# Joined attention visits at equal distances in one decoder layer step

## What is computed

```python
def rms_norm(x, g):
    return x * lax.rsqrt(jnp.mean(x * x, axis=-1, keepdims=True) + 1e-6) * g

def prompt_layer(x, mem, ...):
    z = rms_norm(x, pre_g) @ w_in              # 1024 -> 3072, split in ten parts
    cb, cc, ch, cz, q, k, v, sz, mq, mz = jnp.split(z, points, axis=-1)
    y_conv = cb * short_conv(cc * ch, conv_w) * jax.nn.silu(cz)          # 384 channels
    # blocks of 128 queries on this and the previous 128 keys; 6 query heads, 2 kv heads
    y_swa = swa_attention(q, k_band, v_band, ..., sinks) * jax.nn.silu(sz)
    y_mem = mem_attention(mq, mk, mv) * jax.nn.silu(mz)                  # 4 heads, 256 memory tokens
    y = jnp.concatenate([y_conv, y_swa, y_mem], axis=-1) @ w_out
    return x + rms_norm(y, post_g), ...

def swa_attention(q, k, v, q_pos, k_pos, sinks):
    s = q k^T / 8 - slope * distance, masked to a window of 128
    p = softmax(concatenate([s, sink]))[..., :-1]
    return p v
```

## Time and profile before

| what | us |
|---|---|
| median of 3 runs | 873.94 (872.87 to 874.16) |
| profiled execution, its own time | 872.73 |
| its span, first to last instruction | 870.9 |
| PE busy | 861.3 |
| DVE busy | 470.8 |
| ACT busy | 243.9 |
| POOL busy | 601.1 |

### The profile page before, as it was taken

How to read it: one execution, slowest core, us unless ns; L and a number is a source line. 1 busy time by engine, 2 the same in 40 slices (tenths; PEclk the granted TensorE clock), 3 DMA queues, 4 the chain that set the end, 5 groups by cost and what they waited for, 6 DMA issues and landing times.

```text
span 870.9 us, 13723 instructions
## 1 busy us (share of the span) xinstructions
PE 861.3 (99%) x5228; PEld 709.9 (82%) x5228; DVE 470.8 (54%) x1007; ACT 243.9 (28%) x672; POOL 601.1 (69%) x809
## 2 busy tenths in 40 slices
PE   8999999999999999999999999999999999999997
PEld 8999999998887877777887778777777887787785
DVE  4346688867252527864624346775444053687514
ACT  5433223312121441331311323332121133133111
POOL 4699666439968757727979756653787985776771
PEclk9999999999999999999999999999999999999999
DMA  9457322208357222213646432220543632222242
GB/s 321 177 187 235 103 69 74 74 6 305 126 174 261 98 97 97 73 49 109 256 163 227 171 115 97 65 81 13 181 155 118 232 113 80 73 73 73 58 161 96
DMA packets 38641, 114.01 MB, mean 131 GB/s; under 512 B 6000, under 2 KB 12400, under 8 KB 38160
## 3 DMA queue, kind: packets, MB, share of 16 engines
q1 hardware_dynamic: 37856, 112.02, 37.2%
q10 hardware_dynamic: 720, 1.12, 0.4%
HBM read 103.89 MB, written 10.25 MB: 131 GB/s over the span
## 4 chain that ended last, share of the span: by engine, by line
PE 87%; issue 7%; POOL 4%; DMA 1%; DVE 0%; ACT 0%; SPq 0%; DVEq 0%; POOLq 0%; ACTq 0%
PE pj L646 62%; PE pa L646 22%; POOL w_lo L599 2%; PE pa L798 1%; POOL w_hi L596 1%; PE pa L761 1%; DMA w_raw<-in_weights 1%; POOL rstd L617 1%; PE pa L679 0%; ACT diag L1020 0%; SPq L451 0%; POOL w_lo L611 0%; DVE o_nat L1618 0%; DVEq L244 0%; PE pa L729 0%
## 5 line engine op out<-in xcount | busy, mean ns | idle before, releaser
L599 POOL TENSOR_TENSOR w_lo<-w_raw,w_hi 128x256 fp32r<-128x256 f32 x516 | 411.0, 827 | 10.8
L646 PE MATMUL pj<-h_hi,w_hi 128*128 128x512 f32 (+2 forms) x936 | 337.4, 361 | 2.7 <-POOL w_lo L611 1.7
L646 PE MATMUL pj<-h_hi,w_lo 128*128 128x512 f32 (+2 forms) x936 | 328.6, 351 | 0.0
L646 PE MATMUL pj<-h_lo,w_hi 128*128 128x512 f32 (+2 forms) x936 | 328.0, 350 | 0.0
L596 POOL TENSOR_SCALAR w_hi<-w_raw 128x512 fp32r<-128x512 f32 x258 | 170.1, 677 | 149.7 <-PE pj L646 130.4
L646 PEld LDWEIGHTS pj<-h_hi,w_hi 128*128 128x128 f32 x936 | 176.4, 188 | 39.5 <-issue 17.1
L646 PEld LDWEIGHTS pj<-h_hi,w_lo 128*128 128x128 f32 x936 | 176.4, 188 | 23.5
L646 PEld LDWEIGHTS pj<-h_lo,w_hi 128*128 128x128 f32 x936 | 176.7, 189 | 20.6
L646 PE MATMUL pa<-w_hi,y_hi 128*128 128x512 f32 x160 | 63.8, 398 | 0.0
L646 PE MATMUL pa<-w_lo,y_hi 128*128 128x512 f32 x160 | 62.4, 390 | 0.0
L646 PE MATMUL pa<-w_hi,y_lo 128*128 128x512 f32 x160 | 62.3, 389 | 0.0
(11 more groups left out here) (216 smaller groups left out, 1062.5 us busy)
## 6 DMA issues: line engine op xcount, KB each, us to landing
...
```

What stands on the lines that cost most here:

```text
L599: last = pool.tensor_tensor(w_lo[slot][:, part], raw[:, part], w_hi[slot][:, part].bitcast(F32), ALU.subtract)
L646: return pe.matmul(out, lhsT, rhs, start=start, stop=stop)
```

## The change

The tables of steps change: scores stand at 27, 43, 59, 75 (16 more in quarter 0), so 16 steps apart; both kinds of transposes stand in one visit 9 steps behind (`ATT_T`); the values stand 16 steps behind, which is the step of the next block's scores, and so values of block i and scores of block i+1 are one visit. `nat_turn` moves into the first visit of transposes and writes the right halves of `pa[0]` and `pa[1]` (its sample part `pa[2]`); ACT copies them out in two halves after the block's `mem_pt`. `mem_values` writes `pa[3]` in place of `pa[4]`. `spread_rstd` of the next quarter moves from behind the first output tile into the last visit of values; its means, `diag` and the waits for them move from the third to the second group of convolution tiles. `first_sums` shrinks from 16 matmuls to 2, since DVE adds the eight squares first with four instructions. The count of warm-up matmuls ahead of the first projection stays at 17, over three banks in place of two. `diag` gets memory of its own.

```diff
@@ -200,15 +200,14 @@
-ATT_S = {(q, i): (27, 45, 61, 77)[i] + (16 if q == 0 else 0) for q in range(NQ) for i in range(NBLK)}
-SW_T = {key: s + 8 for key, s in ATT_S.items()}
-MM_T = {key: s + 9 for key, s in ATT_S.items()}
-ATT_V = {key: s + 13 for key, s in ATT_S.items()}
+ATT_S = {(q, i): (27, 43, 59, 75)[i] + (16 if q == 0 else 0) for q in range(NQ) for i in range(NBLK)}
+ATT_T = {key: s + 9 for key, s in ATT_S.items()}
+ATT_V = {key: s + 16 for key, s in ATT_S.items()}
 SM_S, SM_T, SM_V, SM_O = 10, 16, 19, 22
...
-WARM = 9
+WARM = 5
 ROWS_AT = 5
@@ -326,9 +325,8 @@
         x_row = sb("x_row", [P, D])
-        tanh_at = nc.sbuf_base
         tanh_t = sb("tanh_t", [P, 2, TP])
-        diag = at_("diag", [P, TH], tanh_at)
+        diag = sb("diag", [P, TH])
@@ -365,7 +363,8 @@
         row_loaded, res_loaded, xs_loaded, mt_loaded = sems("row_loaded res_loaded xs_loaded mt_loaded")
-        ones_set, x_squares, x_sums, first_his, xts_loaded = sems("ones_set x_squares x_sums first_his xts_loaded")
+        ones_set, x_squares, x_added, x_sums, first_his, xts_loaded = sems(
+            "ones_set x_squares x_added x_sums first_his xts_loaded")
         w0_loaded, w_pieces, k_split, kept, gated = sems("w0_loaded w_pieces k_split kept gated")
@@ -665,23 +664,14 @@
             def nat_turn(q):
-                if q == SAMPLE_OUT + 1:
-                    pe.wait_ge(s_mean, 1)
                 wait_used(pe, (q, "V0", len(chunks(q)) - 1))
+                pe.wait_ge(sw_max, 3 * NBLK * q + 3)
+                for b in range(NBLK):
+                    last = pe.transpose(pa[b // 2][:, (2 + b % 2) * P:(3 + b % 2) * P], v_raw[:, b * P:(b + 1) * P], ident[:])
                 if q == 0:
-                    wait_used(pe, (0, "Q0", 1))
-                if q:
-                    pe.wait_ge(free_dve, FREE_DVE[q - 1, "O0", out_blocks(q - 1) - 1])
-                for b in range(NBLK):
-                    last = pe.transpose(pa[2][:, b * P:(b + 1) * P], v_raw[:, b * P:(b + 1) * P], ident[:])
-                if q == 0:
-                    pe.wait_ge(kept, 1)
                     for g in range(2):
-                        last = pe.transpose(pa[3][0:TG, g * P:(g + 1) * P], v_raw[:, TP + g * TG:TP + (g + 1) * TG],
+                        last = pe.transpose(pa[2][0:TG, (2 + g) * P:(3 + g) * P], v_raw[:, TP + g * TG:TP + (g + 1) * TG],
                                             ident[:])
@@ -732,7 +722,9 @@
                     wait_used(pe, (q, "Q2", len(chunks(q)) - 1))
-                    pe.wait_ge(nat_out, q + 1)
+                    if q == SAMPLE_OUT + 1:
+                        pe.wait_ge(s_mean, 1)
                     if q:
@@ -763,6 +755,8 @@
                 pe.wait_ge(sw_pt, 3 * (NBLK * q + i + 1))
+                if i == 0:
+                    pe.wait_ge(nat_out, q + 1)
                 for kt in range(2):
@@ -805,7 +799,7 @@
                         a = (2 * p + hh) * HD
-                        last = mm(pa[4][HALF_OF[hh], 0:2 * P], mv_sb[:, kt, a:a + HD],
+                        last = mm(pa[3][HALF_OF[hh], 0:2 * P], mv_sb[:, kt, a:a + HD],
                                   mpt[:, hh, kt, :, :].rearrange("p a b -> p (a b)"), kt == 0, kt == 1)
@@ -857,11 +851,9 @@
+                pe.wait_ge(x_added, 1)
                 for b in range(2):
-                    for k in range(KT):
-                        if b == 0 and k % 2 == 0:
-                            pe.wait_ge(x_squares, k // 2 + 1)
-                        last = mm(pa[4][:, b:b + 1], x_sq[:, k, b * P:(b + 1) * P], ones[:, 0:1], k == 0, k == KT - 1)
+                    last = mm(pa[4][:, b:b + 1], x_sq[:, 0, b * P:(b + 1) * P], ones[:, 0:1], True, True)
                 last.then_inc(x_sums, 1)
@@ -886,7 +878,6 @@
                         pe.wait_ge(kept, 2)
-                        pe.wait_ge(nat_out, 1)
                     rows = slice(b * P, (b + 1) * P)
@@ -923,7 +914,7 @@
                     elif b == 3:
-                        pe.wait_ge(mm_pt, 2 * NBLK * (q + 1))
+                        pe.wait_ge(mm_y32, NBLK * (q + 1))
                     else:
@@ -948,7 +939,7 @@
             pe.wait_ge(ones_set, 1)
-            for a in range(2):
+            for a in range(3):
                 for c in range(4):
@@ -974,8 +965,6 @@
                             sample_sums()
-                        if s == 9 and q or s == 21 and q == 0:
-                            nat_turn(q)
                         if q in (1, 2):
@@ -989,9 +978,13 @@
                                 mem_values(q, i)
-                            if s == SW_T[q, i]:
+                                if i == NBLK - 1 and q + 1 < NQ:
+                                    spread_rstd(4, 0, TP, 0, 3 + q + 1)
+                            if s == ATT_T[q, i]:
+                                if i == 0:
+                                    nat_turn(q)
                                 swa_turn(q, i)
-                            if s == MM_T[q, i]:
                                 mem_turn(q, i)
@@ -1009,10 +1002,6 @@
                             out_tile(q, half, kp, b)
-                        if half == 0 and o == 0 and q + 1 < NQ:
-                            pe.wait_ge(mm_y32, NBLK * (q + 1))
-                            spread_rstd(4, 0, TP, 0, 3 + q + 1)
@@ -1093,12 +1082,16 @@
+                act.wait_ge(sw_pt, 3 * NBLK * q + 3)
                 if q:
...
                     for g in range(2):
-                        copy(vn_t[g][:], pa[3][0:TG, g * P:(g + 1) * P])
-                copy(v_sb[:, 1:1 + NBLK, :, :].rearrange("p b v d -> p (b v d)"), pa[2][:]).then_inc(nat_out, 1)
+                        copy(vn_t[g][:], pa[2][0:TG, (2 + g) * P:(3 + g) * P])
+                for a in range(2):
+                    last = copy(v_sb[:, 1 + 2 * a:3 + 2 * a, :, :].rearrange("p b v d -> p (b v d)"), pa[a][:, 2 * P:4 * P])
+                last.then_inc(nat_out, 1)
@@ -1229,17 +1222,15 @@
                             diag_of("m", 0, 2)
-                        if q + 1 < NQ and name == "CB2" and part == 1:
-                            wait_gate(act, (q, "CZ2", len(chunks(q)) - 1))
+                        if q + 1 < NQ and name == "CB1" and part == 1:
+                            act.wait_ge(spread, 3 + q)
                             diag_of(q + 1, 0, NBLK)
...
                             memory_values()
-                        if s == 9 and q or s == 21 and q == 0:
-                            values(q)
                         if q in (1, 2) and s == SM_S:
@@ -1248,8 +1239,10 @@
                                 mem_y_hi(q, i)
-                            if s == MM_T[q, i]:
+                            if s == ATT_T[q, i]:
                                 mem_pt(q, i)
+                                if i == 0:
+                                    values(q)
                             if s == ATT_S[q, i]:
@@ -1572,7 +1565,7 @@
                 wait_gate(dve, (q, f"Z{3 + p}", len(chunks(q)) - 1))
-                dve.scalar_tensor_tensor(out=mo_sum[:], in0=pa[4][:, 0:2 * P], scalar=0.5,
+                dve.scalar_tensor_tensor(out=mo_sum[:], in0=pa[3][:, 0:2 * P], scalar=0.5,
                                          in1=gate[:, 3 + p, gr * 2 * P:(gr + 1) * 2 * P], op0=ALU.mult,
@@ -1654,6 +1647,11 @@
+            for i in range(1, 4):
+                dve.wait_ge(x_squares, i + 1)
+                need(step(dve.tensor_tensor(x_sq[:, 0:2, :], x_sq[:, 0:2, :], x_sq[:, 2 * i:2 * i + 2, :], ALU.add)))
+            dve.tensor_tensor(x_sq[:, 0, :], x_sq[:, 0, :], x_sq[:, 1, :], ALU.add).then_inc(x_added, 1)
             for k in range(KT):
@@ -1713,7 +1711,7 @@
                                 sample_y(q)
-                        if q + 1 < NQ and name == "CH2" and part == 3:
+                        if q + 1 < NQ and name == "CH1" and part == 3:
                             means_of(q + 1)
```

## The result

The changed kernel takes 865.3 us (median of 4 runs, 865.27 to 865.56), the kernel before 873.7 us (4 runs, 872.9 to 874.2): a ratio of 0.990, with a 95% interval of 0.989 to 0.991. The forecast was 863.3 us, range 861.0 to 869.0. The profiled execution of the changed kernel has the median's time, 865.29 us, and a span of 863.5 us, where the kernel before had 872.73 and 870.9: 7.4 us less in the traces, 8.4 in the medians, 10.6 forecast.

The account below looks back on a forecast made before the run. PE, busy 99% of the span, was taken to bound the kernel. Gains of 3.0 + 1.6 + 2.5 + 0.4 + 0.6 + 1.7 + 0.8 = 10.6 us gave 863.3 us as median, range 861.0 to 869.0.

Parts of the forecast that it names:

- sums on PE: Start phase: four one-column passes in place of 32, additions ready on DVE at 19.1 us; 3.0 us gained.
- clock behind the sums: Start phase: the stretch at half clock behind the one-column passes goes; 1.6 us gained, 0 if the clock still falls.
- values with scores: Twelve joined visits: each saves the exit of the values, 0.21 us; 2.5 us gained, bounds 0 and 3.6.
- transposes and V: Sixteen joined visits of transposes, V's in four of them; 0.4 us gained in all, bounds -1 and +1.
- spread in the values' visit: `spread_rstd` in the last visit of values saves one exit in three quarters; 0.6 us gained, bounds 0 and 1.
- POOL's wait at CB2: Means come 16 steps earlier, so PE no longer waits for POOL's late split at CB2; 1.7 us gained, bounds 1.0 and 1.8.
- late normalising: Memory transposes of block 2 no longer catch DVE's last product, in four visits of quarters 1 to 3; 0.8 us gained.
- sums that start by 19.6 us: Start phase, a sign the forecast holds: PE's one-column row with about 0.4 us, starting by 19.6 us.
- late scores behind `o_sum`: Joined visits, a sign of being wrong: first scores over 0.15 us behind `o_sum`'s end minus its cover by memory values.
- Rival 1: DVE's products, slowed by POOL's splits, come late for the transposes in blocks 2 and 3: 4.8 us, 868.1 us; chance 0.15.
- Rival 2: Start gives less: additions take the upper end, clock falls nevertheless; 866.1 us. Chance 0.10 including joints that cost their saving.
- Rival 3: Joined visits of values and scores count as idle and lower PE's clock: 19 us, 882.5 us; chance 0.06.

Follow-up runs that it names:

- experiment 2: The changed kernel with the old sums, 16 matmuls of one column on PE and no additions on DVE: 868.45 us, ratio 0.9935 to the kernel before.
- experiment 5: The changed kernel with the values 13 instead of 16 steps behind the scores, so two visits again: 867.09 us, ratio 0.992 to the kernel before.
- experiment 6: The changed kernel with the window's transposes (and V's) one step ahead of the memory's, splitting the joined visits: 865.56 us, ratio 0.9905 to the kernel before.
- experiment 10: The kernel before with one line changed, DVE making the next quarter's means at CH1, not CH2: 872.41 us against 873.71, ratio 0.998.
- experiment 11: The changed kernel with DVE's `o_sum` of quarter 0 ahead of the second chunk's evacuation: 865.16 us, ratio 0.990 to the kernel before.
- experiment 7: The changed kernel with 56 more wait instructions on PE ahead of the first projection, no more work: 865.57 us, ratio 0.990 to the kernel before.
- experiment 9: The changed kernel with DVE's final rows in quarter 3 held until PE is done with tile K0: 863.94 us, ratio 0.989 to the kernel before.
- experiment 1: The changed kernel run again with no edit: 865.07 us, ratio 0.990 to the kernel before.
- experiment 12: The changed kernel with `o_sum` of quarter 0 ahead of the second evacuation and quarter 3's final rows held until K0 is done: 863.43 us, ratio 0.9883.
- experiment 3: The changed kernel with one DVE addition of 1024 columns and 8 sums on PE: 865.31 us, ratio 0.990 to the kernel before.
- experiment 4: The changed kernel with DVE's four additions behind the first three `h_lo` of the second chunk: 865.48 us, ratio 0.991 to the kernel before.
- experiment 8: The changed kernel with DVE's final rows of the quarter before at step 9 instead of 5: 865.45 us, ratio 0.990 to the kernel before.

## Why the prediction was right, and where it was not

The direction, the order of the terms and most sizes held; the time came out 2.0 us above the forecast. By its terms, as forecast and as measured in the traces:

| term | forecast | measured | from |
|---|---|---|---|
| sums on PE | 3.0 | 3.1 | after, experiment 2 |
| clock behind the sums | 1.6 | 1.5 | experiment 2 |
| values with scores | 2.5 | 2.6 | rows of both traces (0.20 each); experiment 5 (0.23 each) |
| transposes and V | 0.4 | 0.3 | experiment 6, without V |
| spread in the values' visit | 0.6 | 0.0 | below |
| POOL's wait at CB2 | 1.7 | 1.7 | experiment 10 |
| late normalising | 0.8 | 0.8 | four visits 0.20 us shorter; experiment 6 |
| start later | 0 | -0.9 | after, below |
| `o_sum` late in quarter 0 | 0 | -0.8 | after, experiment 11 |
| Q0 of quarter 3 | not seen | -1.2 | experiments 7, 9 |

The measured terms make 7.1 us, the traces show 7.4; 0.3 us I can't place, and the joints alone are open by that much (0.20 or 0.23 us, twelve times).

**Sums.** The step that failed is not their size. The prediction worked out when the additions would be ready (19.1 us; it was 16.9, for they began 2 us earlier and took 3.7 against 4.0) and asked whether PE would wait for them. (Its 0.4 us for handshakes stands in no row; the four additions follow each other without a visible gap.) It said itself that POOL splits beside them, and took the slow price for DVE from that, but left out POOL's half of the same collision. PE waits for POOL there. Its own sign for this, sums that start by 19.6 us, failed: 20.43. The 0.9 us are a net figure. From the first projection to the sums PE took 1.4 us more than before, and began 0.5 us earlier. Of the 1.4, 0.8 are the additions' (the two distances of 0.42 and the 0.22 behind each); 0.5 stand ahead of them (0.32 us at 11.32 and 0.50 at 12.56), beside DVE's own `w_lo`, which began 1.7 us earlier than before; 0.1 is a longer wait for weights. Six traces with the additions and the clock at 1.00 in this phase (after, experiments 1, 5, 9, 11 and 12) take 9.7 to 10.3 us from the end of the wait for weights to the sums, the kernel before 9.0. There is only one such trace without the additions, and in the executions whose clock fell in this phase the stretch takes 10.2 to 10.3 us with them (experiments 3, 4, 6 and 8) and without (experiments 2 and 10). So the place is shown, and the size is good to some tenths.

**Values and scores.** The price of 0.21 us for each, from the exit alone, was right to 0.02. It was split otherwise than it came out: the distance from the memory part of the values to the next thing is 0.97 us in the joined visit and was 0.96 ahead of a projection, so what went is the 0.11 behind the values and the 0.09 in front of the scores. The cover of `o_sum` was worked out for one chunk of 512 columns and counted twelve times; in quarter 0 it is another sequence, with the second chunk's two products ahead. That is the mis-sized term: two places of the kind "each us of lateness costs one", 0.12 and 0.65 us. The prediction had named late scores behind `o_sum` as a sign of being wrong, and there it came.

**Spread.** Forecast: "saves one exit in three quarters, 0.2 x 3". The trace of after, last values of quarter 1, and of before, behind the first output matmul:

```profile
395.59 1.13 PE L645 MATMUL pa<-diag,ones 128*128 128x512 f32 x2
396.15 0.80 PE L645 MATMUL pj<-h_hi,w_hi 128*128 128x512 f32 x1
396.78 0.39 PE L645 MATMUL pj<-h_lo,w_hi 128*128 128x512 f32 x1
```

```profile
206.04 1.02 PE L646 MATMUL pa<-diag,ones 128*128 128x512 f32 x2
206.49 0.80 PE L646 MATMUL pa<-w_hi,y_hi 128*128 128x512 f32 x1
207.13 0.40 PE L646 MATMUL pa<-w_lo,y_hi 128*128 128x512 f32 x1
```

The dear part is the distance behind the spread, 0.63 us, and it moved with it; 0.56 inside the visit against 0.45 alone is the 0.11 behind the values that I had counted as saved, and the 0.10 at their end stayed here as well. Above what PE would need without the spread this is 0.56 + 0.63 - 0.34 = 0.85 us after and 0.45 + 0.64 - 0.23 = 0.86 us before.

**Rivals.** Rival 1 (DVE late for the transposes) did not come in the changed kernel: POOL slows the products as it said (1.04 us), but they end over 1 us ahead of the transposes. Its mechanism is real, as experiment 10 shows without the even distances. Rival 2 came in part: the start gave 0.9 us less, mostly by waits for POOL and not by its two reasons. Rival 3, the clock in joined visits, did not come: 1.00 over 286 to 400 us with visits of 4.3 us in it, and after up to 2.1 us of transposes in a row. The rule on transposes that the prediction set beside it (the Trainium skill, TensorE: Matmul & The Clock Gate, Part 4: PE-mode transpose) cost nothing here at that length.

**What was not asked.** The prediction followed waits between engines, but neither the loads nor the fetch of instructions. 28 matmul instructions fewer on PE are also a shift of later fetches against the loads. No entry of the prediction's closing list would have shown it. So the time fell inside the range with three losses outside the sum (0.9, 0.8 and 1.2 us) and a fourth term, the spread, at nothing in place of 0.6; the range had been drawn for other reasons.
